# Two attention pipelines set back by one step and a weight-conversion look-ahead shortened by one chunk, in a two-block transformer kernel

## The reference

```
h = h + 0.5 * rmsnorm(swiglu(rmsnorm(h)), g)
u = rmsnorm(h, g);  proj = u @ w_in
oa = neighbourhood_attention(qa, ka, va)        # called na in the kernel, 8 heads
ob = sliding_window_attention(qb, kb, vb, sink) # called sw, 8 heads
oc = differential_attention(qc, kc, vc, lam)    # called diff: softmax 1 - lam * softmax 2, 4 heads
merged = sum_n sigmoid(gate_n) * ([oa, ob, oc][n] @ w_branch[n])
h = h + rmsnorm(merged @ w_out, g)
h = h + 0.5 * rmsnorm(swiglu(rmsnorm(h)), g)
```

## Time and profile before

| | us |
|---|---|
| median of three runs | 1707.87 |
| the profiled execution: its own time | 1707.87 |
| its span, first to last instruction | 1706.1 |
| PE busy | 1599.4 |
| DVE busy | 1067.8 |
| ACT busy | 853.9 |
| POOL busy | 120.0 |

### The profile page before, as it was taken

One profiled execution on the slowest core, in us unless ns is written; L12 is line 12 of the kernel. 1 busy time (PEld: TensorE's weight loads), 2 busy tenths in 40 slices (PEclk: granted clock), 3 DMA queues, 4 the chain that ended last, 5 costly groups with the idle time before them and its releaser, 6 DMA issues.

```text
span 1706.1 us, 21800 instructions
## 1 busy us (share of the span) xinstructions
PE 1599.4 (94%) x7796; PEld 1317.9 (77%) x7796; DVE 1067.8 (63%) x1792; ACT 853.9 (50%) x1487; POOL 120.0 (7%) x157
## 2 busy tenths in 40 slices
PE   1778989999999999999999999999999999999998
PEld 1557768778888777878778887888778787778886
DVE  5778577666655646567666556665555567665653
ACT  0346546645444555555454445444455655454442
POOL 3011001100000300002100000000020001200000
PEclk9989989999999999999999999999999999999999
DMA  9665257336556553445565555555482354655552
GB/s 285 206 234 185 95 180 230 109 112 206 176 185 196 149 174 125 129 140 164 185 202 173 193 189 184 189 175 192 158 223 94 121 161 138 201 185 187 176 193 76
DMA packets 155336, 293.27 MB, mean 172 GB/s; under 512 B 10214, under 2 KB 23316, under 8 KB 155228
## 3 DMA queue, kind: packets, MB, share of 16 engines
q1 hardware_dynamic: 149312, 276.60, 50.1%
q0 software_dynamic: 4800, 12.29, 3.1%
q10 hardware_dynamic: 1116, 2.99, 0.5%
HBM read 290.77 MB, written 1.06 MB: 171 GB/s over the span
## 4 chain that ended last, share of the span: by engine, by line
PE 80%; DVE 8%; DMA 5%; ACT 3%; issue 3%; POOL 1%; SPq 0%; DVEq 0%; POOLq 0%; ACTq 0%
PE pb L434 75%; PE pb L438 4%; DMA raw<-in_w_in 3%; DVE wl L1293 2%; DVE acc L1290 1%; DMA raw<-in_w_ada 1%; POOL st L2046 1%; ACT wh L805 1%; DVE xt_l L1290 1%; ACT xt_h L805 1%; DVE dg L1287 0%; DVE xt_l L1293 0%; ACT pb L805 0%; DVE h L1290 0%; DVE B L1293 0%
## 5 line engine op out<-in xcount | busy, mean ns | idle before, releaser
L805 ACT ACTIVATE wh<-raw 128x1024 fp32r<-128x1024 f32 (+1 forms) x484 | 504.8, 1053 | 437.3 <-PE pb L434 378.0
L1293 DVE TENSOR_TENSOR wl<-raw,wh 128x1024 fp32r<-128x1024 f32 (+1 forms) x484 | 579.0, 1216 | 199.1 <-ACT wh L805 195.7
L434 PE MATMUL pb<-wh,xt_h 128*128 128x512 f32 (+2 forms) x1536 | 593.2, 386 | 14.3 <-ACT wh L805 12.3
L434 PE MATMUL pb<-wl,xt_h 128*128 128x512 f32 (+2 forms) x1536 | 585.0, 381 | 18.6 <-DVE wl L1293 18.4
L434 PE MATMUL pb<-wh,xt_l 128*128 128x512 f32 (+2 forms) x1536 | 585.7, 381 | 0.6 <-DVE xt_l L1290 0.4
L434 PEld LDWEIGHTS pb<-wl,xt_h 128*128 128x128 f32 x1536 | 291.5, 190 | 73.3 <-DVE wl L1293 23.6
L434 PEld LDWEIGHTS pb<-wh,xt_h 128*128 128x128 f32 x1536 | 291.5, 190 | 71.7 <-ACT xt_h L805 13.0
L434 PEld LDWEIGHTS pb<-wh,xt_l 128*128 128x128 f32 x1536 | 291.0, 189 | 59.2 <-DVE xt_l L1290 6.5
L434 PE MATMUL pb<-wh,big_h 128*128 128x512 f32 x352 | 138.9, 395 | 0.0
L434 PE MATMUL pb<-wl,big_h 128*128 128x512 f32 x352 | 138.3, 393 | 0.0
L434 PE MATMUL pb<-wh,big_l 128*128 128x512 f32 x352 | 137.2, 390 | 0.0
(11 more groups left out here) (205 smaller groups left out, 1480.0 us busy)
## 6 DMA issues: line engine op xcount, KB each, us to landing
raw<-in_ffn_w_gu SPq DMA_DIRECT2D x176, 512.0 KB, 4.5
raw<-in_w_in SPq DMA_DIRECT2D x148, 512.0 KB, 4.5
raw<-in_ffn_w_down SPq DMA_DIRECT2D x88, 512.0 KB, 3.7
raw<-in_w_ada SPq DMA_DIRECT2D x48, 512.0 KB, 5.4
raw<-in_w_out SPq DMA_DIRECT2D x32, 512.0 KB, 4.2
raw<-in_w_branch SPq DMA_DIRECT2D x24, 512.0 KB, 3.6
raw<-in_w_in SPq DMA_DIRECT2D x8, 416.0 KB, 4.0
G<-in_na_rpb POOLq DMA_DIRECT2D x32, 96.0 KB, 8.6
```

The lines of the kernel that those rows point to most:

```text
L434: return e.matmul(o, a, b, start=start, stop=stop)
L805: return e.activation(o, a, func, **kw)
L1293: return e.tensor_tensor(o, a, b, op)
```

## The change

Three numbers change. ACT's look-ahead goes from four chunks to three, so that both engines now use `AHEAD` = 3. The lag of `na`, `sw` and `diff` goes from 3 to 2, as it is for the other two; these attentions have eleven steps in place of twelve. The ring of probabilities in the second block has three buffers in place of four.

```diff
-    def __init__(self, plan, ahead):
-        self.plan, self.ahead, self.taken, self.next, self.freed = plan, ahead, 0, 0, 0
+    def __init__(self, plan):
+        self.plan, self.taken, self.next, self.freed = plan, 0, 0, 0
...
-            if split is not None and not (split <= c + self.ahead and split - NW < self.freed):
+            if split is not None and not (split <= c + AHEAD and split - NW < self.freed):
...
-    pb2 = [sb(f"p2_{i}", [128, 512], F, mx) for i in range(4)]
+    pb2 = [sb(f"p2_{i}", [128, 512], F, mx) for i in range(3)]
...
-    LAG = {"moba": 2, "mla": 2, "na": 3, "sw": 3, "diff": 3}
...
-            lag = LAG[name]
-            for k in range(NU + lag + 1):
-                if lag <= k < NU + lag:
-                    u = k - lag
+            for k in range(NU + 3):
+                if 2 <= k <= NU + 1:
+                    u = k - 2
...
-                if k > lag:
-                    i = k - lag - 1
+                if k >= 3:
+                    i = k - 3
...
-                               [("eva", (s, "va"), 1)]), NU + 4)
+                               [("eva", (s, "va"), 1)]), NU + 3)
...
-        stream = Stream(plan, AHEAD + 1)
+        stream = Stream(plan)
...
-        stream = Stream(plan, AHEAD)
+        stream = Stream(plan)
```

More of the change, by code:

```diff
@@ L739, in mixer @@
             side.add(attention("sw", l, [("qk", (s, "swq"), 2), ("qk", (s, "swk"), 0)],
-                               [("eva", (s, "kvb"), 1)]), NU + 4)
+                               [("eva", (s, "kvb"), 1)]), NU + 3)
             side.over(12)
@@ L764, in mixer @@
             side.add(attention("diff", l, [("qk", (s, "dfq"), 2), ("qk", (s, "dfk"), 2)],
-                               [("eva", (s, "vc"), 1)]), NU + 4)
+                               [("eva", (s, "vc"), 1)]), NU + 3)
             side.over(12)
@@ L923, in attention @@
                                 bias=m).then_inc(*up("es", *a, k, j))
-                if name == "diff" and k > lag and (k - lag - 1) % 4 == 3:
-                    t = (k - lag - 1) // 4
+                if name == "diff" and k >= 3 and (k - 3) % 4 == 3:
+                    t = (k - 3) // 4
                     v = temp(("dfsq", l, t, 3))
@@ L1174, in mixer @@
             turn_heads((s, "nak"), 4, kts[0], 128, old=H[1][0])
-            side.add(attention("na", l), NU + 4)
+            side.add(attention("na", l), NU + 3)
             if l == 0:
@@ L1197, in mixer @@
             side.add(sw_steps(), 5)
-            side.add(attention("sw", l, sinks=True), NU + 4)
+            side.add(attention("sw", l, sinks=True), NU + 3)
             side.over(12)
@@ L1238, in mixer @@
             turn_heads((s, "dfk"), 4, kts[0], 128)
-            side.add(attention("diff", l), NU + 4)
+            side.add(attention("diff", l), NU + 3)
             side.over(12)
@@ L1456, in attention @@
                     tails.popleft()()
[L1457 to L1461, removed]
+                if k >= 3 and (k - 3) % 4 == 3:
+                    t = (k - 3) // 4
+                    w.wait_ge(*at("pv", *a, k - 3))
+                    w.wait_ge(*at("exp", *a, k - 3, 1))
                     o_dst(t, banks[7], sums[t])
-                while tails and k == NU + lag:
+                while tails and k == NU + 2:
                     tails.popleft()()
@@ L1915, in mixer @@
             turn_heads(4)
-            side.add(attention("na", l, by_sums(lambda t: O[:, t, :], ("na", l)), [("nab", l)]), NU + 4)
+            side.add(attention("na", l, by_sums(lambda t: O[:, t, :], ("na", l)), [("nab", l)]), NU + 3)
             if l == 0:
@@ L1936, in mixer @@
             side.add(sw_steps(), 5)
-            side.add(attention("sw", l, by_sums(lambda t: B[:, t, 0:512], ("sw", l)), [("sink",)]), NU + 4)
+            side.add(attention("sw", l, by_sums(lambda t: B[:, t, 0:512], ("sw", l)), [("sink",)]), NU + 3)
             side.over(12)
@@ L2010, in diff_out @@
                 tails.extend([sums_, scale_])
-            side.add(attention("diff", l, diff_out, tails=tails), NU + 4)
+            side.add(attention("diff", l, diff_out, tails=tails), NU + 3)
             side.over(12)
```

## The result

The changed kernel takes 1725.9 us (median of six runs, 1724.4 to 1728.2) against 1710.5 for the kernel before, run beside it: a ratio of 1.0097, interval 1.0079 to 1.0114. It is slower by 15.3 us by the medians. The profiled execution took 1725.93 us (span 1724.1), 18.1 more than that of before, 18.0 by the spans.

A forecast was written before the change was run, and what follows sets the result against it. PE, busy 94% of the span, was taken as the bound. Terms -0.4 + 5.1 + 1.0 + 8.4 - 2.1 - 1.2 = +10.8 us on 1707.87 gave 1718.7, rounded to 1718.5; 8-in-10 range 1703 to 1727.

The forecast's parts named there:

- layer 0, start-up and MoBA: First layer: 5.5 us gained in the start-up, 5.1 lost in the MoBA loop, net -0.4 us.
- layer 1, MoBA: Second layer's MoBA loop: DVE and ACT take turns, last maxima and PE 5.1 us late; bounds 0 and 8.
- MLA, both layers: MLA attention: full chunks lie between, exposed delay about 0.5 us per layer, +1.0 us.
- The head start: Start-up: evacuations stand behind one chunk less, kb near 105 us, PE 7.6 us earlier at first scores; 5.5 counted.
- In the first layer the order is the same: First layer's MoBA: same loop order as the second layer, so same 5.1 us loss, spending the 5.5 us gained.
- Lag 2 in diff: loss: Differential attention: PE waits for DVE's combination in a 4.5 us loop; 4.2 us per layer, 8.4 in all.
- The POOL term: Diff: DVE's factor operation slowed beside POOL's additions, now on the path; 0.5 us per layer.
- The small ones: Mixer starts: waits for va go, -2.1 us; sw: 0.58 us wait goes, -1.2; lag 2 in na and sw: 0.
- (a): Rival: PE has more chunks in hand in MoBA and diff, head start and small gains stay; 1697 us, chance 0.08.
- (b): Rival: only MoBA loses, the diff loop of 4.5 us hides under PE's 4.68; 1710 us, chance 0.20.
- (d): Rival: nothing to measure, queues have a step in hand and transfers limit the start-up; 1708 us, chance 0.12.
- (c): Rival: the wait spreads in sw, about 2.2 us in six places per layer, +20 us; 1738 us, chance 0.07.

The follow-up runs named there:

- ahead3_block1: Kernel before with ACT's look-ahead 3 in the first block alone, 4 from the first feed-forward on; lags and buffers unchanged: 1715.4 us, 1.0031.
- after_pool_late: Changed kernel with POOL's two additions of the second branch's first half held until DVE's second maximum of diff's fifth unit: 1725.4 us, 1.0101 to the kernel before.
- lag2_only: Kernel before with only the lag of na, sw and diff cut to 2 and three probability buffers; ACT's look-ahead stays 4: 1708.5 us, 0.9994.
- ahead3_diff: Kernel before with ACT's look-ahead 3 only through each mixer's second branch, where differential attention runs; lag 3, four buffers: 1720.8 us, 1.0073.
- ahead3_only: Kernel before with only ACT's look-ahead cut from 4 to 3; lags 3 and four buffers stay: 1726.2 us, 1.0101.

## Why the prediction was wrong

It named the direction and too small a size: 10.8 us forecast, 15.3 measured by the medians, 18.1 in the profiled execution. Its steps, in the changed kernel's profile, by how much later PE reaches the same place:

| step | forecast | measured |
|---|---|---|
| layer 0, start-up and MoBA | -0.4 | +5.7 (-4.5 at the first scores, then +10.2) |
| layer 1, MoBA | +5.1 | +5.1 |
| MLA, both layers | +1.0 | -3.0 |
| mixer starts and sw | -3.3 | about -2.0 |
| diff, both | +8.4 | +11.5 (5.5 and 6.0) |
| the rest | 0 | +0.8 |

The 7.3 us between 10.8 and 18.1 are 6.1 more in layer 0, 3.1 more in diff and 2.1 more in the starts, sw and the rest, less 4.0 in MLA.

**The head start** was right in kind and size: kb at 104.18 (said: near 105), PE 4.5 us earlier at the first scores, 5.9 to 7.6 in six others with the same start-up (said: 7.6, of which the sum took 5.5). The profile of before is the earliest of nine with look-ahead 4 there (130.25 to 133.78, median 131.87); the seven with look-ahead 3 have a median of 124.09, 7.8 us less. The way was partly wrong: PE's wait of 7.90 us shrank to 6.90, not to 4, and the gain came at the later waits.

**"In the first layer the order is the same"** is the step that failed in the first block. The order of the attention's own steps is; but DVE has four pairs of w_ada operations (1.5 us each) inside the loop in layer 0 and two in layer 1. Cutting three of the pairs, from 1.53 to 0.48 us each, shortens the stretch by 1.4 us in the kernel before, which had room for part of them, and by 6.0 with look-ahead 3. Of the 6.0 us a wait of 3.07 for the exponentials, which is gone, is about the 3.2 us cut; the other 2.9 are PE's busy time (36.79 to 33.85 us, at clocks of 0.88 and 0.95). Whether the clock would have cost this by itself was not tried. So 5.1 became 9.5. In layer 1 the step held: the last maxima come 321.62 - 286.86 = 34.76 us behind the first scores, before 313.16 - 283.50 = 29.66, that is 5.1 us later as said.

MLA is a term that had the wrong sign: +1.0 forecast, -3.0 measured. I had looked for waits there. The waits hardly changed; the half clock did. PE is busy for 28.58 and 28.64 us in these stretches, before for 30.04 and 30.03, and over all the kernels run the MLA stretch is 30.8 to 31.7 us long at a clock of 1.00 and 32.5 to 33.1 at 0.95:

```profile
164.50:197.54 33.04, 30.04 (x187) 26.48 (x186) 16.91 (x49) 20.82 (x55) 0.61 (x1) 0.95 0.28 97
```

```profile
170.20:201.32 31.12, 28.58 (x186) 24.82 (x186) 16.15 (x47) 20.38 (x55) 0.61 (x1) 1.00 0.28 90
```

Why the clock stays full there in one execution and not in another is open. The first block as a whole, 5.7 forecast, was met (5.3 us, 3.2 to 7.3, in ahead3_block1; 7.4 in the changed kernel's profile), but by luck, through errors that cancel.

**"Lag 2 in diff: loss"** is the step that failed in the second block: its loop is right and its cause is not. The turn is 4.52 us (said: 4.5). In the changed kernel the fourth combination is late by 2.07 us, the seventh hidden and the eighth late by 1.52 in the first mixer and 0.47 in the second (said: 0.6 and 0.5 for POOL, 0.9, 2.2). With POOL out of the way, in after_pool_late, the waits are 0.64, 0.90 and 2.12: the adding up turn by turn was right. But the loop is closed by lo waiting for hi, which the look-ahead brings; with lag 3 the combination's spare step only moves PE's wait to the output of the first four units, 3.1 us, since DVE as a whole is late. lag2_only lost nothing, and ahead3_diff lost 12.5 us.

**The POOL term** is the one mis-sized: 0.5 us per diff, measured 0.67 - 0.22 and 1.45 - 0.48, together 1.42. I had the rule of the Trainium skill, page "SBUF — State Buffer", section "SBUF: two separate sides", that a DVE operation with two SBUF inputs and a POOL operation exclude each other and the later one stands still until the other ends, and took one row instead. The traces agree with the rule in three places: the factor operation ends at 776.98 with the first addition, the combination meets the second addition, and the lo conversion in after_pool_late meets the moved one. With 1.42 the fourth combination is 2.0 us late, and PE waited 2.07. The extra 1.8 us for two mixers leave 1.3 us of the 11.5 unexplained by combinations. They are not in waits that the profile names: even at full clock and with POOL moved, PE is busy for 50.10 us in this stretch, in lag2_only for 49.31.

**The small ones.** The waits of 1.28 and 0.95 for va (2.2 together, not 2.1) and of 0.58 in sw went, as said, but 1.3 of the 3.3 us did not come back as time; na and sw cost nothing by lag 2 (lag2_only even reaches diff 2 us earlier per mixer, from sw). Not foreseen: PE waits 0.86 us for POOL at the merges, 0.3 before. The rivals are out: diff did lose, against (a), (b) and (d), and sw lost 2.3 us at most (in ahead3_only), not the 20 of (c). What stays open is how much of the MoBA loss is the clock, and the spread: the same MoBA program in layer 1 cost 5.1 to 7.8 us in different executions, and the changed kernel's own profile lost 2.7 us more than its medians.

## What to carry to other kernels

When two engines work on the same stream of tiles one after the other, look at the lead of the first over the second before the depth of either: here equal look-aheads turned each step of an attention into a chain through both, and one chunk of lead took that away even when both were shorter. When a slack goes, price everything that had been hiding in it, in each place by itself, however alike the places look. A change with two parts wants one run for each part before either is blamed.

## What the runs showed of the hardware

PE fell to its half clock (1.2 GHz) behind waits as short as 0.9 to 1.1 us: in the changed kernel such stretches, without the last few us of the span, make 64.8 us against 34.1 before, among them 13.7 us from 134.8 on, behind the wait of 1.11 us at 132.63. In the kernel before 3.4 us from 1326.1 on follow a wait of 0.88 at 1324.11.

```profile
132.63 0.41 PE L437 MATMUL pb<-cst,pb 128*128 128x128 f32 x2 [1.11 <-ACT pb L803]
```

```profile
135.00:155.00 20.00, 20.00 (x69) 14.32 (x68) 14.22 (x36) 12.05 (x31) 1.75 (x1) 0.66 0.46 135
```

At half clock a matmul of 512 columns follows the one before by 0.43 us in place of 0.23. But the same lost clock was worth nothing inside a loop that other engines pace (54.88 us at 1.00, 54.85 at 0.97), and cost about half its length where PE was the bound again (1.6 us for 3.4 in after_pool_late, 1.4 us of busy time for 3.4 in MLA). With lag 3 and its one late wait it was in between: the two diff stretches of ahead3_only are 54.89 us at 0.94 and 53.69 at 0.97. Not every such wait is followed by it: behind 1.78 us at 173.46 the clock stayed at 1.00.
